# Routed experts in a decoder trunk: the gather of two expert groups in one product of 256 columns

## The reference

```
scores = sigmoid(h @ w_router)                       # 256 x 64
top_e  = top_k(scores + b_router, 8)
top_w  = scores[top_e] / sum(scores[top_e]) * 2.5
expert e, for its tokens:  y = (silu(x @ w_eg[e]) * (x @ w_eu[e])) @ w_ed[e]   # 1024 -> 256 -> 1024
out    = sum over the 8 experts of top_w * y  +  (silu(h @ w_sg) * (h @ w_su)) @ w_sd
h      = h + gate * out
```

## Time and profile before

| | us |
|---|---|
| median of 3 runs | 1393.61 |
| lowest, highest | 1393.27, 1396.72 |
| the profiled execution | 1396.53 |
| its span | 1394.8 |

### The profile page before, as it was taken

How to read it: one execution, slowest core, us unless ns; L and a number is a source line. 1 busy time by engine, 2 the same in 40 slices (tenths; PEclk the granted TensorE clock), 3 DMA queues, 4 the chain that set the end, 5 groups by cost and what they waited for, 6 DMA issues and landing times.

```text
span 1394.8 us, 20069 instructions
## 1 busy us (share of the span) xinstructions
PE 1338.6 (96%) x8011; PEld 783.8 (56%) x8011; DVE 428.8 (31%) x969; ACT 268.4 (19%) x534; POOL 32.1 (2%) x82
## 2 busy tenths in 40 slices
PE   5998989999999999999899899899999999999997
PEld 1887865465444444444388788754564444444442
DVE  1799672101111111111183698611111111111111
ACT  2222531110111111011133563410110111111100
POOL 4000000001000000000000000000010000000000
PEclk9999999999999999999999999999999999999999
DMA  9999666999999999999999602579999999999996
GB/s 381 390 421 421 266 247 260 385 421 361 423 420 421 422 421 421 421 421 421 421 417 420 252 1 90 220 307 383 420 362 422 420 421 422 421 421 422 420 421 286
DMA packets 71774, 512.94 MB, mean 368 GB/s; under 512 B 8240, under 2 KB 8448, under 8 KB 9728
## 3 DMA queue, kind: packets, MB, share of 16 engines
q1 hardware_dynamic: 70560, 509.64, 88.6%
q0 software_dynamic: 832, 1.39, 0.5%
q10 hardware_dynamic: 288, 0.61, 0.1%
HBM read 510.55 MB, written 1.05 MB: 367 GB/s over the span
## 4 chain that ended last, share of the span: by engine, by line
PE 80%; DMA 8%; DVE 7%; ACT 2%; issue 2%; SPq 1%; DVEq 0%; ACTq 0%
PE PS L987 24%; PE PS L977 13%; PE PS L995 12%; PE PS L1011 11%; PE PS L565 6%; DMA ring<-in_w_in_a_units 4%; DMA ring<-in_w_exp 4%; DVE ring L614 2%; PE PS L737 2%; PE PS L1023 2%; SPq L1397 1%; PE PS L692 1%; PE PS L1852 1%; PE PS L1032 1%; PE PS L716 1%
## 5 line engine op out<-in xcount | busy, mean ns | idle before, releaser
L987 PE MATMUL PS<-ring,scratch 128*32 128x512 f32 (+2 forms) x2176 | 353.7, 593 | 6.7 <-DMA ring<-in_w_exp 5.3
L987 PEld LDWEIGHTS PS<-ring,scratch 128*32 128x32 f32 (+2 forms) x2176 | 111.0, 122 | 242.3 <-issue 240.6
L1342 DVE TENSOR_TENSOR scratch<-PS,gate_row 128x512 f32<-128x512 f32 x100 | 69.2, 692 | 462.3 <-PE PS L995 462.3
L977 PEld LDWEIGHTS PS<-scratch,u 128*128 128x128 f32 x1600 | 186.2, 194 | 38.4 <-issue 36.5
L977 PE MATMUL PS<-scratch,u 128*128 128x128 f32 x1600 | 195.4, 281 | 1.4 <-ACT scratch L1206 1.4
L995 PE MATMUL PS<-ring,scratch 128*32 128x512 f32 (+2 forms) x1088 | 182.2, 596 | 3.4 <-DMA ring<-in_w_exp 2.2
L1011 PE MATMUL PS<-scratch 128*128 128x512 f32 x384 | 172.7, 592 | 0.0
L565 PE MATMUL PS<-ring,uT 128*128 128x256 f32 x672 | 148.6, 380 | 3.6 <-DMA ring<-in_w_in_a_units 3.4
L1214 ACT ACTIVATE scratch<-PS 128x256 f32<-128x256 f32 x50 | 19.2, 384 | 672.9 <-PE PS L987 672.9
L565 PEld LDWEIGHTS PS<-ring,uT 128*128 128x128 f32 x672 | 126.3, 190 | 22.6 <-issue 4.2
L1330 DVE TENSOR_TENSOR scratch<-scratch,PS 128x256 f32<-128x256 f32 x50 | 21.1, 422 | 329.7 <-ACT scratch L1214 329.7
(11 more groups left out here) (346 smaller groups left out, 856.9 us busy)
## 6 DMA issues: line engine op xcount, KB each, us to landing
ring<-in_w_exp SPq DMA_DIRECT2D x384, 1024.0 KB, 16.4
ring<-in_w_ada_columns SPq DMA_DIRECT2D x48, 1024.0 KB, 25.6
ring<-in_w_in_a_units SPq DMA_DIRECT2D x12, 1024.0 KB, 27.5
ring<-in_w_ada_units SPq DMA_DIRECT2D x8, 1024.0 KB, 16.1
ring<-in_w_cmp_units SPq DMA_DIRECT2D x8, 1024.0 KB, 24.0
ring<-in_w_sh_units SPq DMA_DIRECT2D x6, 1024.0 KB, 13.7
ring<-in_w_kv_b_units SPq DMA_DIRECT2D x6, 1024.0 KB, 22.4
ring<-in_w_o_a_units SPq DMA_DIRECT2D x4, 1024.0 KB, 26.4
```

The source lines that it names most:

```text
L977: mm = pe_.matmul(PS[:, bank, i * w:(i + 1) * w], u[:, t, k * P:(k + 1) * P], hot[:, t, :], start=(t == 0), stop=(t == NT - 1))
L987: mm = pe_.matmul(PS[places, GU, :], x[:, kk, places], gate_and_up, start=(kk == 0), stop=(kk == KC - 1))
L1342: dve.tensor_tensor(y_rows[:, half * 512:(half + 1) * 512], PS[:, Y0 + half, :], gate_row[:, half * 512:(half + 1) * 512], ALU.mult).then_ ...
```

## The change

Group 0 gathers as before, but into buffers of its own names (`x_first`, `one_hot_first`). From group 1 on, groups are gathered in twos: groups 1 and 2 are pair 0, groups 3 and 4 pair 1, and so on to groups 23 and 24, pair 11. The one-hot matrices of a pair lie side by side, 256 columns, and one product picks the rows of both. A pair's gather is cut in four quarters of two feature chunks, each 4 products of 256 columns and one PSUM bank. All four quarters of pair 0 run in group 0, into banks 4, 0, 1 and 2. The quarters of pair p run two in group 2p-1 and two in group 2p, into banks 4 and 7. Group 23 gathers nothing. The buffers of gathered rows and of one-hot matrices are twice as large. VectorE makes the one-hot matrices of two groups in every even group, and that of group 2 ahead of the first group.

```diff
-        x_pair = [cut(0, [KC, P]), cut(1024, [KC, P])]
-        one_hot = [cut(2048, [NT, P]), cut(2304, [NT, P])]
+        x_pairs = [cut(0, [KC, 2 * P]), cut(6528, [KC, 2 * P])]
+        one_hots = [cut(2048, [NT, 2 * P]), cut(S0 + 1696, [NT, 2 * P])]
+        x_first, one_hot_first = cut(6528, [KC, P]), cut(S0 + 1696, [NT, P])
...
-        def gather_bank(g, half):
-            return Y0 + 1 if half and g > 1 else GATHER
+        def gathers_in(g):
+            n = len(GROUPS)
+            if g == 0:
+                return [(0, quarter, bank) for quarter, bank in enumerate((GATHER, 0, 1, 2))]
+            pair = (g + 1) // 2
+            return [(pair, 2 * (1 - g % 2) + i, (GATHER, Y0 + 1)[i]) for i in range(2)] if 2 * pair + 1 < n else []
+
+        def gathered_by(g):
+            return 2 + sum(len(gathers_in(i)) for i in range(g + 1))
...
-                if not last:
-                    pe_.wait_ge(*by_group("onehot_ready", layer, g + 2))
-                    if g == SHARED_AT[0] + 1:
-                        pe_.wait_ge(routing["shared_act"], layer + 1)
-                    elif g == SHARED_AT[1] + 1:
-                        pe_.wait_ge(routing["shared_hid"], layer + 1)
-                    pe_gather(pe_, one_hot[(g + 1) % 2], range(0, 4)).then_inc(group_sem["gathered"], 1)
-                    if g:
+                if g == SHARED_AT[0] + 1:
+                    pe_.wait_ge(routing["shared_act"], layer + 1)
+                elif g == SHARED_AT[1] + 1:
+                    pe_.wait_ge(routing["shared_hid"], layer + 1)
+                for pair, quarter, bank in gathers_in(g):
+                    pe_.wait_ge(*by_group("onehot_ready", layer, 2 * pair + 3))
+                    if bank == Y0 + 1:
                         pe_.wait_ge(*by_group("y_ready", layer, 2 * g))
-                    else:
-                        pe_.wait_ge(*by_group("x_ready", layer, 3))
-                    pe_gather(pe_, one_hot[(g + 1) % 2], range(4, 8), gather_bank(g + 1, 1)
+                    pe_gather(pe_, one_hots[pair % 2], (2 * quarter, 2 * quarter + 1), bank
                               ).then_inc(group_sem["gathered"], 1)
...
-                if not last:
-                    pe_.wait_ge(*by_group("x_ready", layer, 2 * g + 4))
+                pe_.wait_ge(*by_group("x_ready", layer, gathered_by(g)))
...
-            def copy_x(g, half):
-                act.wait_ge(*by_group("gathered", layer, 2 * g + half + 1))
-                act.activation(x_pair[g % 2][:, 4 * half:4 * half + 4, :].rearrange("p k s -> p (k s)"),
-                               PS[:, gather_bank(g, half), :], ACT.Copy).then_inc(group_sem["x_ready"], 1)
+            def copy_x(n, pair, quarter, bank):
+                act.wait_ge(*by_group("gathered", layer, n))
+                act.activation(x_pairs[pair % 2][:, 2 * quarter:2 * quarter + 2, :].rearrange("p k s -> p (k s)"),
+                               PS[:, bank, :], ACT.Copy).then_inc(group_sem["x_ready"], 1)
...
+            done(hot(2, slot_ranked), group_sem["onehot_ready"])
             done(hot_weighted(0), group_sem["hot_w_ready"])
...
-                if g + 2 < len(GROUPS):
-                    done(hot(g + 2, slot_ranked), group_sem["onehot_ready"])
+                if g % 2 == 0 and g + 4 < len(GROUPS):
+                    for following in (g + 3, g + 4):
+                        done(hot(following, slot_ranked), group_sem["onehot_ready"])
```

More of the change, by code:

```diff
@@ L335, in of_keys, with side_of, x_of, one_hot_of @@
             return rows.rearrange("p t (a b c) -> p t a b c", a=2, b=2)[:, :, :, 1, 0:H]
-        x_pair = [cut(0, [KC, P]), cut(1024, [KC, P])]
-        one_hot = [cut(2048, [NT, P]), cut(2304, [NT, P])]
+        x_pairs = [cut(0, [KC, 2 * P]), cut(6528, [KC, 2 * P])]
+        one_hots = [cut(2048, [NT, 2 * P]), cut(S0 + 1696, [NT, 2 * P])]
+        x_first, one_hot_first = cut(6528, [KC, P]), cut(S0 + 1696, [NT, P])
+        def side_of(g):
+            return slice((g - 1) % 2 * P, ((g - 1) % 2 + 1) * P)
+        def x_of(g):
+            return x_pairs[(g - 1) // 2 % 2][:, :, side_of(g)] if g else x_first
+        def one_hot_of(g):
+            return one_hots[(g - 1) // 2 % 2][:, :, side_of(g)] if g else one_hot_first
         hot_w = cut(2560, [NT, P])
@@ L1079, in pe_moe @@
             pe_.wait_ge(*by_group("onehot_ready", layer, 1))
-            pe_gather(pe_, one_hot[0], range(0, 4)).then_inc(group_sem["gathered"], 1)
+            pe_gather(pe_, one_hot_first, range(0, 4)).then_inc(group_sem["gathered"], 1)
             pe_.wait_ge(routing["unranked_copied"], layer + 1)
@@ L1092, in pe_moe @@
             pe_.wait_ge(*by_group("x_ready", layer, 1))
-            pe_gather(pe_, one_hot[0], range(4, 8)).then_inc(group_sem["gathered"], 1)
+            pe_gather(pe_, one_hot_first, range(4, 8)).then_inc(group_sem["gathered"], 1)
             def item_ends():
@@ L1114, in pe_moe @@
                 last = g == len(GROUPS) - 1
-                pe_.wait_ge(*by_group("x_ready", layer, 2 * g + 2))
+                pe_.wait_ge(*by_group("x_ready", layer, gathered_by(g - 1)))
                 for half in range(2):
@@ L1119, in pe_moe @@
                     slots = [slot_no(gate_up_unit(layer, g, i, half)) for i in range(len(group))]
-                    pe_gate_up(pe_, slots, x_pair[g % 2], tiles, half
+                    pe_gate_up(pe_, slots, x_of(g), tiles, half
                                ).then_inc(group_sem["gu_out" if half else "gu_half_out"], 1)
@@ L1202, in act_moe @@
                  routing["unranked_copied"])
-            def copy_x(g, half):
-                act.wait_ge(*by_group("gathered", layer, 2 * g + half + 1))
-                act.activation(x_pair[g % 2][:, 4 * half:4 * half + 4, :].rearrange("p k s -> p (k s)"),
-                               PS[:, gather_bank(g, half), :], ACT.Copy).then_inc(group_sem["x_ready"], 1)
             for half in range(2):
-                copy_x(0, half)
+                act.wait_ge(*by_group("gathered", layer, half + 1))
+                act.activation(x_first[:, 4 * half:4 * half + 4, :].rearrange("p k s -> p (k s)"),
+                               PS[:, GATHER, :], ACT.Copy).then_inc(group_sem["x_ready"], 1)
+            def copy_x(n, pair, quarter, bank):
+                act.wait_ge(*by_group("gathered", layer, n))
+                act.activation(x_pairs[pair % 2][:, 2 * quarter:2 * quarter + 2, :].rearrange("p k s -> p (k s)"),
+                               PS[:, bank, :], ACT.Copy).then_inc(group_sem["x_ready"], 1)
             for g in range(len(GROUPS)):
-                last = g == len(GROUPS) - 1
                 act.wait_ge(*by_group("gu_out", layer, g + 1))
                 act.activation(gate_act, PS[:, GU, 0:D_EXP], ACT.Silu).then_inc(group_sem["gate_ready"], 1)
-                if not last:
-                    for half in range(2):
-                        copy_x(g + 1, half)
+                for i, (pair, quarter, bank) in enumerate(gathers_in(g)):
+                    copy_x(gathered_by(g - 1) + i + 1, pair, quarter, bank)
                 act.wait_ge(*by_group("turned", layer, g + 1))
@@ L1275, in hot @@
                 for r, n, at, w in runs(g):
-                    ins = dve.tensor_tensor(places(one_hot[g % 2], n, at, w),
+                    ins = dve.tensor_tensor(places(one_hot_of(g), n, at, w),
                                             iota[:, 1:1 + w].unsqueeze(1).unsqueeze(1).to_broadcast([P, NT, n, w]),
@@ L1282, in hot_weighted @@
                 for r, n, at, w in runs(g):
-                    ins = dve.tensor_tensor(places(hot_w, n, at, w), places(one_hot[g % 2], n, at, w),
+                    ins = dve.tensor_tensor(places(hot_w, n, at, w), places(one_hot_of(g), n, at, w),
                                             weight_ranked[:, :, r:r + n].unsqueeze(3).to_broadcast([P, NT, n, w]), ALU.mult)
```

## The result

The changed kernel is slower: a median of 1407.4 us over 11 runs (1397.96 to 1412.42) against 1393.61 us (1392.41 to 1396.72), a ratio of 1.0095 with a 95% interval of 1.007 to 1.012. On another chip it was 1401.57 (1397.89 to 1426.7, 12 runs) against 1393.78 (1391.8 to 1404.79, 23 runs), ratio 1.0039 (1.0015 to 1.0064). So the loss is clear of noise on both, but its size is not the same. The forecast was 1395.9, in a range of 1391 to 1400.

What follows compares the result with a forecast made beforehand. It took the load stream behind each layer's last hole as the bound: +2.27 in group 0 less 5 x 0.22 gives +1.17, about +1.2 us per layer, +2.3 in all, from 1393.61 to 1395.9 us, range 1391 to 1400.

Steps and rivals of the forecast that it cites:

- What bounds the experts' parts: In both layers' experts' parts, the end is the last hole's end plus a 421 GB/s load stream that cannot be pressed.
- the last hole: Last gap in each layer's loads, 334 to 346 us in layer 0; it ends when group 6's first half releases slots.
- The gain in later groups is worth nothing: Behind the last hole, TensorE's 0.22 us saved per group only makes it wait longer for loads in group 24.
- Two terms of the sum: Group 0's four quarters cost +2.27 us; the gathers of groups 1 to 5 save 0.22 us each; +1.17 per layer.
- the sum is a difference and holds for both: Whole kernel: the +2.3 us applies alike to the profiled execution (1396.53 to 1398.8) and the median (1393.61 to 1395.9).
- its clock is full there: Reading of the earlier profile's slices: where TensorE is busy, nearly everywhere, its clock is full; no size given.
- it only lengthens the wait for the loads: Group 23 has no gather, so 3.67 - 1.1 us go; group 24 then waits 6 us and more, not 3.8.
- a little slower: Rival: products of 256 columns save nothing in the gathers; +2.27 to +2.9 us per layer, 1398.1 to 1399.4 us; chance 0.12.
- A new wait in every group: Rival: each group's second quarter or turn waits 0.69 us for ScalarE's copy; +6.2 us per layer, 1406 us; chance 0.07.
- slower a chance of 0.17: Outcome for the whole kernel: a measured time over 1397.8 us, which counts as slower; chance 0.17.

Runs made afterwards that it cites:

- with the clock held up: Both kernels with unread products in the attention of layer 1, ahead of each routing and in group 24: before 1388.85 us, changed 1392.67 us.
- the lag of 2.3 us alone: The kernel before with 20 more instructions of 128 columns (ten unread products) in group 0 of each layer: median 1409.01 us.
- the shortened gather in both layers: The kernel before with group 23 gathering one product in place of eight per half, in both layers: 1465.3 us.
- the larger lag: The kernel before with 32 more instructions of 128 columns (3.7 us) in group 0: median 1403.20 us.
- two lag kernels: The kernel before with 3.7 us of unread products in group 0, 1403.20 us; and with 2.3 us there plus unread products in TensorE's long waits, 1394.52 us.
- the late lag: The kernel before with unread products in layer 1's attention and ahead of each routing, plus 20 instructions (2.3 us) in group 10 of each layer: 1390.85 us.

## Why the prediction was wrong

**What bounds the experts' parts: right.** The stream behind the last hole runs at 419 to 421 GB/s in every profile, TensorE waits for loads in group 24 in all of them, and the gain in groups 7 to 23 brings nothing: with the clock held up the changed kernel's parts are longer, not shorter. "The gain in later groups is worth nothing" is shown only in that direction; a lag there is not free (1.3 of 2.3 us, of which 0.5 is in the stream of loads and the rest one late load per layer). The packets of the two first profiles say the same without the clock: counted from the start of group 0, the loads after run 1.6 to 1.9 us behind those of before from the last hole to the end of either layer, and the last one lands 1.55 and 1.73 us later.

**Two terms of the sum were mis-sized**, by one cause. The gather gains 0.11 us per group and not 0.22, and group 0 pays 2.38 and not 2.27. The 216 ns for 256 columns were right: 32 instructions take 7.01 us and 16 take 3.56, so 16 more take 3.45. But a gather takes 0.11 us more than its instructions at that distance, and so does today's: 32 in 3.67 and 16 in 1.89, so 16 more take 1.78 us, 111 ns each. The 115 ns that I took for 128 columns had the 0.11 us in them, the 216 ns from the shared expert had not. +2.38 - 5 x 0.11 = +1.83 per layer in place of +1.17. Measured with the clock held up: +1.7 and +1.9. The mechanism was right and would have given 1397.3 for 1395.9. The estimate from the Trainium skill (TensorE: Matmul & The Clock Gate, "Wait — 56ns, not 53.3ns?") had been 218 and 112 ns and a gain of 0.08; the trace has 216 and 111 and a gain of 0.11, so at 128 columns the page was nearer than the average that I went by.

**The step that failed** is the one that closes the sum: "the sum is a difference and holds for both". It adds up what the change does to the gathers and takes it that everything else costs what it did, above all that TensorE's clock stays where it was ("its clock is full there"). Of the clock there is no term in the sum, and no reason but that reading is given. The 9s of the earlier trace rows do not bear it out: a 9 stands for 90% and more, and the stretch 800 to 810 of before had 0.74. With the clock held up in four places the difference between the kernels is 3.8 us, near the sum; without, it was 13.8 and 7.8 us at the median on two chips. So 4 to 10 us of the loss are clock, in the routing, the attention and group 24, differently placed from run to run. The largest piece in the profiled pair is the 6.8 us between the experts' parts. The runs' times follow their mean granted clock: 0.995 at 1391.8 and 0.985 at 1404.8 us for the kernel before, about 1.0 to 1.3 us for 0.001. The changed kernel's runs have 0.977 to 0.990 (and one 0.945), those of before 0.985 to 0.996, most of them 0.989 and more. At one mean clock the two kernels hardly differ (at 0.989 four changed runs have 1397.9 to 1398.4 us, seven of before 1396.6 to 1400.1), less than the 3.8 us. A fall in group 24, which the changed kernel has in its profiles and the kernel before has not, lowers the mean but costs little, as the next paragraph shows; that this is the whole reason is argued.

**A second step failed** in the same way, on group 24: "it only lengthens the wait for the loads". The wait is not idle time that costs nothing. The clock falls to the lower level in it, and 32 instructions behind it take 5.35 us for 3.64 (5.62 in layer 1). After the 1.1 us of the next wait are eaten, the down product starts 0.67 us behind the last landing in layer 0 and 0.98 in layer 1, before 0.14; so 0.5 and 0.8 us are left of it, parts of the +2.1 and +2.6. The Trainium skill says in general ("Loop structure matters more than you think" in TensorE: Matmul & The Clock Gate) that a wait for a DMA between bursts of products lets TensorE go cold; the waits of 5.8 us here agree.

**What stays open** is why the change makes these falls likelier. The long wait in group 24 is not needed: the lag of 2.3 us alone had a median of 1409.01. Nor did it do this in the one profile with the shortened gather in both layers: the wait in group 24 was 5.26 us and the stretch between the experts' parts 215.49. And the kernel before has such runs too (5 of 23 at 1399 us or more in that comparison). That a shift of everything behind group 0 moves the weak stretches of work into a worse place for the clock fits this, but no run shows it, and the larger lag neither confirms nor excludes it.

Of the rivals, "a little slower" named the right direction; its ground, 256 columns that save nothing, was not the case. Its price was also too low by its own ground: quarters at 2 x 115 ns take 7.36 us, which is +2.7 and not +2.27. "A new wait in every group" did not come: there is none in 243.11 to 246.67. I had given slower a chance of 0.17, and none of my cases had the clock in it.

## What to carry to other kernels

Where a stream of loads sets the end, look for its last hole. What TensorE does ahead of it counts in full, a gain behind it counts for nothing, a lag behind it for a part, and work moved from behind it to ahead of it (here a burst of four quarters in group 0) is a loss even where the total shrinks. Before timing small changes, look at the granted clock in stretches of little work and at the spread of single runs: a kernel with a few long waits can lose more by the clock than the change is worth, and products that nothing reads in those waits bought 5.7 us here and made differences of 2 us measurable. When two profiles differ, compare the granted clock of stretches whose code is the same first.

## What the runs showed of the hardware

In a row of float32 products of 128x256 the next instruction starts 216 ns later, in the shared expert as in the gather; at 128 columns it is 111 to 112 ns. A gather takes 0.11 us more than that, whether it has 16 or 32 instructions (3.56 and 7.01 us at 256 columns, 1.89 and 3.67 at 128).

In the traces of these runs TensorE's clock is full or half at every moment. A wait of 2.7 us in group 24 left it at 1.00 in the profile of before (672 to 690), one of 5.8 did not (0.81); but one of 2.4 in the lag kernel did not either (0.71 over 5 us). So the length of the one wait does not decide it. The attention, with the same code, had a stretch of 10 us at 1.00 in one run and at 0.51 in another, which is about 5 us of work.

The loads of 1 MB land 2.5 us apart behind the last hole, but not all. In every profile kept here one or more in this stretch of either layer come 3 to 4 us behind the one before, at no fixed place. Where that falls among the last units, TensorE waits for it: 2.30 and 2.66 us ahead of the last down product of layer 0 in two lag kernels, 1.94 and 1.89 in the late lag, at most 1.1 elsewhere. The cause is not shown.
